# MLP of a two-layer encoder: two kinds of weight block sums move from accumulating DMAs to VectorE, up blocks go to other buffers, and the first chunk's work on h is spread further

## What is computed

```python
def sqrelu_mlp(h, w_up, w_down):
    return jnp.square(jax.nn.relu(h @ w_up)) @ w_down

for i in range(DEPTH):
    ...
    h = rmsnorm(x, g_ffn_pre[i])
    x = x + rmsnorm(sqrelu_mlp(h, mlp_w_up[i], mlp_w_down[i]), g_ffn_post[i])
```

## Time and profile before

| | us |
|---|---|
| median of 3 runs | 1190.64 (1189.11 to 1191.31) |
| profiled execution, its own time | 1189.05 |
| span in that profile | 1187.3 |
| TensorE busy (matmuls) | 1126.0 |
| VectorE busy | 912.2 |
| ScalarE busy | 763.1 |
| GpSimd busy | 317.0 |

### The profile page before, as it was taken

One profiled execution on the slowest core, in us unless ns is written; L12 is line 12 of the kernel. 1 busy time (PEld: TensorE's weight loads), 2 busy tenths in 40 slices (PEclk: granted clock), 3 DMA queues, 4 the chain that ended last, 5 costly groups with the idle time before them and its releaser, 6 DMA issues. The chain is left out here.

```text
span 1187.3 us, 18208 instructions
## 1 busy us (share of the span) xinstructions
PE 1126.0 (95%) x6462; PEld 976.4 (82%) x6462; DVE 912.2 (77%) x1328; ACT 763.1 (64%) x1266; POOL 317.0 (27%) x289
## 2 busy tenths in 40 slices
PE   8999999999899999899999999999998899899987
PEld 7788789887797897887977888879777887887876
DVE  5899965798586685679789888875897685585678
ACT  6778867556583583565787777775565673663754
POOL 5688850312022022112421111100311121030014
PEclk9999999999999999999999999999999999999999
DMA  5322134269579589575124322324669578687663
GB/s 162 105 60 71 36 109 106 72 186 200 143 174 214 137 188 206 120 206 107 54 54 103 75 70 62 97 64 122 199 143 210 131 180 186 159 177 171 157 175 103
DMA packets 142708, 157.22 MB, mean 132 GB/s; under 512 B 6269, under 2 KB 108669, under 8 KB 142122
## 3 DMA queue, kind: packets, MB, share of 16 engines
q1 hardware_dynamic: 112300, 109.68, 30.0%
q0 software_dynamic: 30256, 46.41, 23.6%
q10 hardware_dynamic: 78, 0.16, 0.0%
HBM read 147.58 MB, written 6.29 MB: 130 GB/s over the span
## 5 line engine op out<-in xcount | busy, mean ns | idle before, releaser
L2174 DVE TENSOR_TENSOR wlo<-mraw,whi 128x1024 fp32r<-128x1024 f32 x212 | 255.6, 1224 | 149.0 <-ACT whi L1509 148.9
L1509 ACT ACTIVATE whi<-mraw 128x1024 fp32r<-128x1024 f32 x212 | 218.1, 1053 | 195.2 <-DMA mraw<-in_mlp_w_down 108.3
L1203 PE MATMUL psum<-whi,aop_hi 128*128 128x512 f32 x448 | 178.6, 399 | 19.9 <-DVE wlo L2174 16.0
L1204 PE MATMUL psum<-wlo,aop_hi 128*128 128x512 f32 x448 | 174.7, 390 | 0.0
L1205 PE MATMUL psum<-whi,aop_lo 128*128 128x512 f32 x448 | 174.6, 390 | 0.0
L873 PE MATMUL psum<-hhi,whi 128*128 128x512 f32 x376 | 150.8, 401 | 0.8 <-DVE wlo L2163 0.5
L875 PE MATMUL psum<-hhi,wlo 128*128 128x512 f32 x376 | 147.0, 391 | 0.0
L874 PE MATMUL psum<-hlo,whi 128*128 128x512 f32 x376 | 146.8, 390 | 0.0
L1203 PEld LDWEIGHTS psum<-whi,aop_hi 128*128 128x128 f32 x448 | 84.1, 188 | 48.9 <-DVE wlo L2174 21.9
L1189 PE MATMUL psum<-hhi,whi 128*128 128x256 f32 x384 | 110.5, 288 | 14.4 <-DVE wlo L2174 12.1
L1190 PE MATMUL psum<-xlo,whi 128*128 128x256 f32 x384 | 109.3, 285 | 0.0
(11 more groups left out here) (314 smaller groups left out, 2807.9 us busy)
## 6 DMA issues: line engine op xcount, KB each, us to landing
mraw<-in_mlp_w_up SPq DMA_DIRECT2D x64, 512.0 KB, 6.8
mraw<-in_mlp_w_down SPq DMA_DIRECT2D x64, 512.0 KB, 4.9
mraw<-in_mlp_w_down POOLq DMA_DIRECT2D x60, 512.0 KB, 7.3
mraw<-in_mlp_w_up POOLq DMA_DIRECT2D x24, 512.0 KB, 10.7
wraw<-in_conv_pw_w SPq DMA_DIRECT2D x20, 512.0 KB, 4.5
wraw<-in_attn_w_in SPq DMA_DIRECT2D x16, 512.0 KB, 4.8
x_copy<-xT SPq DMA_DIRECT2D x2, 2048.0 KB, 7.4
xT<-x_copy SPq DMA_DIRECT2D x2, 2048.0 KB, 11.3
```

What stands on the lines that cost most here:

```text
L1203: pe.matmul(o, ah, wh, start=kt == 0 and (not kept or c == 0), stop=False)
L1204: pe.matmul(o, ah, wl, start=False, stop=False)
L1509: a.activation(split_unit(whi, e), raw_unit(l, c, e_), ACT.Copy).then_inc(s["m_hi"], 1)
L2174: d.tensor_tensor(split_unit(wlo, e), raw_unit(l, c, e_), split_unit(whi, e).bitcast(F32), ALU.subtract).then_inc(s["m_ready"], 1)
```

## The change

It has four parts.

1. **Sums.** Down P6 of chunks 0 to 2 and down P4 of chunks 1 and 2 are VectorE adds of blocks that lie in SBUF (`add_block`, now with the product as an argument), no longer accumulating DMAs. P4 of chunks 0 and 3 stays a DMA.
2. **Buffers and loads.** From chunk 2 on the up blocks B11 and B12 swap slots (B11 into that of down B21, B12 into that of down B22); B11 of chunk 1 and B12 of later ones are loaded behind P6's add, B11 of later ones behind P4's. `FIRST_SLOTS` of layer 0 is another permutation.
3. **GpSimd's order.** Chunk 0: P7, P5, P4. Later chunks: the up sums P7 and P4 first, then down P7h0, P5, P7h1. Chunk 3's P4 last.
4. **First chunk.** The 8 passes over h, the four sums and the forms' halves are placed later and further apart; three forms are finished by VectorE in the up part of chunk 1 or just ahead of it.

The functions `t_nth` and `v4_nth` only count semaphores anew. The core of the diff:

```diff
-FIRST_SLOTS = ((3, 1, 2, 0), (0, 1, 2, 3))
+FIRST_SLOTS = ((2, 3, 1, 0), (0, 1, 2, 3))
...
     d = down_slots(l, c - 1)
-    return d[B22], d[B12], d[B21], d[B11]
+    if c == 1:
+        return d[B22], d[B12], d[B21], d[B11]
+    return d[B21], d[B12], d[B22], d[B11]
...
-                    for b, at_ in ((B12, 3), (B11, 7), (B21, 11), (B22, 13)):
+                    for h in range(2):
+                        if c == 1:
+                            up_half(c, B12, h, n + 3 + h)
+                    for h in range(2):
+                        sp.wait_ge(s["t_sum"], t_nth(l, c - 1, "down", h))
+                        up_half(c, B11 if c == 1 else B12, h, n + 7 + h)
+                    for h in range(2):
+                        if c > 1:
+                            sp.wait_ge(s["t_sum"], t_nth(l, c - 1, "down", 2 + h))
+                            up_half(c, B11, h, n + 9 + h)
+                    for b, at_ in ((B21, 11), (B22, 13)):
...
-                for c in range(CHUNKS):
+                for h in range(2):
+                    add_down(l, 0, P7, h)
+                for i in (P5, P4):
                     for h in range(2):
-                        if c:
-                            add_up(l, c, P4, h)
-                        add_down(l, c, P7, h)
+                        add_down(l, 0, i, h)
+                for c in range(1, CHUNKS):
+                    for i in (P7, P4):
+                        for h in range(2):
+                            add_up(l, c, i, h)
+                    add_down(l, c, P7, 0)
                     for h in range(2):
                         add_down(l, c, P5, h)
-                    for h in range(2 if c < CHUNKS - 1 else 0):
-                        add_down(l, c, P6, h)
-                    for h in range(2 if c < CHUNKS - 1 else 0):
-                        add_up(l, c + 1, P7, h)
-                    for h in range(2):
-                        add_down(l, c, P4, h)
+                    add_down(l, c, P7, 1)
+                for h in range(2):
+                    add_down(l, CHUNKS - 1, P4, h)
...
-                for j, (kept_, forms) in enumerate(((P1, (A11, S7)), (P2, (A12,)), (P5, (S2,)), (None, (S5, A22)),
-                                                    (P6, (S4,)))):
+                for j, (kept_, forms) in enumerate(((P1, ()), (P2, ()), (P5, ()), (None, (A11, S7)), (P6, (A12, S2)))):
...
-            def add_block(l, h):
-
-                c = CHUNKS - 1
+            def add_block(l, c, i, h):
+
                 r = down_slots(l, c)
...
+                source, last_use = {P6: (B22, P5), P4: (B21, P6)}[i]
+                dve.wait_ge(*loaded(r[source], h, 2 * (CHUNKS * l + c) + 2))
+                dve.wait_ge(s["m_ready"], MLP_UNITS * l + DOWN[c] + DOWN_AT[c][last_use] + h + 1)
                 dve.wait_ge(v4_sum[h], 16 * v4_nth(l, c, "down", P5))
                 half = slice(h * D, (h + 1) * D)
                 to = mraw[:, r[B11], half]
...
+                d.tensor_tensor(to, to, mraw[:, r[source], half], ALU.add).then_inc(s["t_sum"], 1)
```

More of the change, by code:

```diff
@@ L91, in t_nth @@
 def t_nth(l, c, phase, k):
-    return 14 * l + (4 * c - 4 if phase == "up" else 12) + k + 1
+    return 24 * l + (8 * c - 6 if c else 0) + (4 if c and phase == "down" else 0) + k + 1
 def v4_nth(l, c, phase, i):
-    return 14 * l + 4 * c + (0 if phase == "up" else {P5: 1, P6: 2, P4: 3 if c < CHUNKS - 1 else 2}[i])
+    return 9 * l + 2 * c + (1 if phase == "up" else {P5: 2 if c else 1, P4: 3 if c else 2}[i])
 def v_nth(l, c, phase):
@@ L1502, in m_hi @@
                         act.wait_ge(v7_sum[h], 16 * v7_nth(l, c, "down", h))
-                    elif i == P6 and c == CHUNKS - 1:
+                    elif i == P6:
                         act.wait_ge(s["t_sum"], t_nth(l, c, "down", h))
-                    elif i in (P5, P6, P4):
+                    elif i == P4 and 0 < c < CHUNKS - 1:
+                        act.wait_ge(s["t_sum"], t_nth(l, c, "down", 2 + h))
+                    elif i in (P5, P4):
                         act.wait_ge(v4_sum[h], 16 * v4_nth(l, c, "down", i))
@@ L1889, in mlp @@
                 for i in range(4):
+                    if i == 3:
+                        m_hi(l, 8)
                     up_square(g, 2 * i)
@@ L1918, in mlp @@
                 m_hi(l, n + 16)
+                for form in (S5, A22, S4):
+                    form_hi_of(l, form)
                 for c in range(1, CHUNKS):
@@ L2518, in add_block @@
                 to = mraw[:, r[B11], half]
-                d.tensor_tensor(to, to, mraw[:, r[B22], half], ALU.add).then_inc(s["t_sum"], 1)
+                d.tensor_tensor(to, to, mraw[:, r[source], half], ALU.add).then_inc(s["t_sum"], 1)
             def add_up_block(l, c, i, h):
@@ L2657, in first_up @@
                 s_lo(g, 1)
-                for k in range(2):
-                    h_whole(l, k)
+                h_whole(l, 0)
+                h_whole(l, 1)
                 m_lo(l, 7)
@@ L2666, in first_up @@
                 relu(g, 6)
+                m_lo(l, 8)
                 s_lo(g, 2)
-                for k in range(2, 5):
-                    h_whole(l, k)
-                m_lo(l, 8)
+                h_whole(l, 2)
                 s7(g, 3)
+                a1_lo(g, 3)
                 m_lo(l, 9)
-                a1_lo(g, 3)
-                for k in range(5, KB):
-                    h_whole(l, k)
                 m_lo(l, 10)
@@ L2678, in first_up @@
                 s_sums(g, 3)
+                m_lo(l, 11)
                 a_lo(g, 3)
-                m_lo(l, 11)
                 s_lo(g, 3)
-                h_sum(l, S5)
+                h_whole(l, 3)
             def first_down(l):
@@ L2686, in first_down @@
                 m_lo(l, n + 4)
+                h_whole(l, 4)
+                h_whole(l, 5)
+                m_lo(l, n + 5)
+                add_block(l, 0, P6, 0)
+                m_lo(l, n + 6)
+                add_block(l, 0, P6, 1)
+                m_lo(l, n + 7)
+                h_whole(l, 6)
+                h_whole(l, 7)
+                m_lo(l, n + 8)
+                h_sum(l, S5)
+                m_lo(l, n + 9)
                 h_sum(l, S7)
-                m_lo(l, n + 5)
+                m_lo(l, n + 10)
                 h_sum(l, S2)
-                m_lo(l, n + 6)
                 h_sum(l, S4)
-                m_lo(l, n + 7)
+                m_lo(l, n + 11)
                 form_rest(l, A11)
-                m_lo(l, n + 8)
+                m_lo(l, n + 12)
                 form_rest(l, S7)
-                m_lo(l, n + 9)
+                m_lo(l, n + 13)
                 form_rest(l, A12)
-                m_lo(l, n + 10)
-                form_rest(l, S2)
-                m_lo(l, n + 11)
-                form_rest(l, S5)
-                m_lo(l, n + 12)
-                form_rest(l, A22)
-                m_lo(l, n + 13)
-                form_rest(l, S4)
                 m_lo(l, n + 14)
                 add_up_block(l, 1, P6, 0)
+                form_rest(l, S2)
                 m_lo(l, n + 15)
@@ L2710, in first_down @@
                 m_lo(l, n + 16)
+                form_rest(l, S5)
             def up_chunk(l, c):
                 g, n = CHUNKS * l + c, BASE[c]
-                for e in range(3, 8):
+                m_lo(l, n + 3)
+                if c == 1:
+                    form_rest(l, A22)
+                m_lo(l, n + 4)
+                if c == 1:
+                    form_rest(l, S4)
+                for e in range(5, 8):
                     m_lo(l, n + e)
@@ L2749, in down_chunk @@
                 m_lo(l, n + 5)
+                add_block(l, c, P6, 0)
                 m_lo(l, n + 6)
+                add_block(l, c, P6, 1)
                 add_product(g, P2)
@@ L2754, in down_chunk @@
                 m_lo(l, n + 9)
+                add_block(l, c, P4, 0)
                 add_product(g, P5)
                 m_lo(l, n + 10)
+                add_block(l, c, P4, 1)
                 m_lo(l, n + 11)
```

15 lines of the change are left out of this document (5 added, 10 removed).

## The result

The change takes 1137.84 us (median of 4 runs, 1136.93 to 1139.56), the kernel before in the same job 1189.88 (4 runs, 1188.16 to 1191.31). The ratio is 0.9565, 95% interval 0.9546 to 0.9583: 52 us or 4.35% faster. The profiled execution took 1139.56 us, the slowest of its four, with a span of 1137.8. Against the profiled pair of before (1189.05, span 1187.3) the gain is 49.5 us; the sum had said 46.3.

A forecast was written before the change was run, and what follows sets the result against it. The prediction took a queue of accumulating DMAs, not an engine, to bound the kernel. Terms 11.4 + 18.6 + 9.3 + 7.0 = 46.3 us off 1189.05 gave 1142.8, plus 1.6 to the median: 1144.4 us, range 1139.5 to 1157.

The forecast's parts named there:

- What bounds the kernel: MLP: TensorE's waits come from a queue of accumulating DMAs, not an engine; 50 us are there to win.
- The 0.27 us charged to each wait: TensorE's waits before MLP matmuls: each costs 0.27 us beyond its row; 39.8 us in 38 waits make 50 us.
- Down P4 and the next up part: Down P4 in chunks 1 and 2 and the next chunk's start: both kinds of wait go, winning 11.4 us.
- Up P4: Up chunks, P4 and P3: the sum is issued earlier and lands in 7 to 8 us, winning 18.6 us.
- 20.6, less 2 left: 18.6: Up P4 term: waits of 12.1 and 5.5 us plus 11 x 0.27 make 20.6; 2 us were expected to remain.
- The limit of 10.6: Up part: nothing is lost if the up P4 sum lands within 10.6 us of TensorE beginning the chunk.
- First chunk: First down chunk of each layer: waits at P2h1, P5h0 and P4's halves go, winning 9.3 us with 0.5 left.
- Last down half: Last down halves: P5's sums go ahead of P7h1's, ending `acc` and `wlo` waits, winning 7.0 us with 1.4 left.
- At nothing: Layer 0's first blocks in other slots, and B11 of chunks 2 and 3 loaded after P4's add: no cost.
- Rival 1: Up P4 sum stays slow and units lag in the packed first chunk: 8.5 us more, 1153 us; chance 20%.
- Rival 2: Start of up chunks: B12, loaded after P6's add, delays up P7's sum and TensorE waits; 1169 us; chance 8%.
- Rival 3: GpSimd cannot issue sums while VectorE adds, so they start only in VectorE's pauses; about 1198 us, slower; chance 2%.

The follow-up runs named there:

- e1: Kernel before with only GpSimd's sums reordered (down P4 ahead of the next up P7, P5 ahead of P7's second half); 1164.05 us, ratio 0.98.
- e8: The change with the up P4 sum's first half issued one unit later in layer 0, two in layer 1; 1153.84 us, ratio 0.9698.
- e10: Kernel before with GpSimd's new order, new form work places and both plain loads late in both layers, no new VectorE adds; 1139.2 us, ratio 0.9576.
- e9: Kernel before with only plain loads for the next down part issued later, one in layer 0, two in layer 1; 1187.65 us, ratio 0.9983.
- e12: e3 with the two plain loads behind the up P4 sum issued late, as in e10; 1147.56 us, ratio 0.9661.
- e4: The change with GpSimd's old order in later chunks: up P4 and down P7 sums alternating, both P7 halves ahead of P5; 1145.29 us, ratio 0.9639.
- e6: The change with `wlo` of down chunks 1 and 2 made in 2 pieces in layer 0, 8 in layer 1; 1147.53 us, ratio 0.9644.
- e3: The change with down P4 of chunks 1 and 2 summed by GpSimd DMAs again, ahead of the next up P7 sums; 1165.98 us, ratio 0.9809.
- e11: e3 with the two pairs of sums swapped, the next chunk's up P7 ahead of down P4; 1181.17 us, ratio 0.9933.
- e5: Kernel before with GpSimd's new order and the new places of the form work, all block sums still DMAs; 1152.38 us, ratio 0.9691.

## Why the prediction was right, and where it was off

**What bounds the kernel.** Right: with the waits for sums gone TensorE is busy 98% of the span, and the 22.4 us on VectorE cost nothing that shows. (TensorE's busy time, expected to stay near 1126 us, fell to 1116.8: first matmuls behind a wait are longer, and there was half clock.) The 0.27 us charged to each wait on top of its row held too: 39.8 us of waits less the 1.2 left, and 9.2 for the surcharge on 34 of them, make 47.8 against 49.8 in the parts.

**Down P4 and the next up part: right**, 11.9 us against 11.4. The diagnosis, a queue of accumulating DMAs, held, but adds on VectorE are only one way to mend it: e1 gets the same down parts by order alone.

**Up P4: the term that was mis-sized**, 21.7 us against 18.6. "20.6, less 2 left: 18.6" is the step of the sum that failed: 0.4 us were left and not 2, and the 20.6 was itself 1.6 short. The issue was forecast 0.7 us into the part and came at 0.7 to 1.5, the sum was wanted within 10.6, and it landed at 6.5 to 9.6. Even in up 1, issued at 3.6 and 3.9 and so later than the 2.4 forecast, it landed at 9.5 and 10.9: 0.4 us lost in one part. The limit of 10.6 was exact: landings at 10.2 (e8) and 10.5 (e10) cost nothing, 10.8 (e10) 0.3, and 10.9 (the change) 0.4. The prediction took landings of 7 to 8 us; four of the six took 5.8 to 5.9, the others 7.0 and 8.1. It kept 2 us because it could not tell why landings were 10 us in one place and 5.9 in another, though it named the two close loads in the earlier trace rows as a suspect. e9, e10 and e12 show it was them. The Trainium skill, "DMA: Bandwidth & Descriptors", section "Queues, rings and completion order", says that each DMA engine goes round among the queues that have work, packet by packet; landings of 5.9 to 7.3, 8.4 to 8.6 and 9.5 to 10.5 us with none, one and two plain loads close behind agree. The estimate from the fit in the same page of the Trainium skill, section "Anatomy of one DMA — SWDGE (gpsimd) path", that the prediction had weighed (3.2 us for 512 KB) is not seen: the quickest block sum of all these traces took 5.4 us (e1). The 1.6 us by which the 20.6 was short were a sixth delay at P4 and P3, in up 1 of layer 0, which stands in no wait row because TensorE was running at half clock (last section).

**First chunk: right**, 9.3 us against 9.3, with waits of 0.3 and 0.4 left at P5h0. But what waits there is ScalarE's copy of P1's product, not VectorE.

**Last down half: right**, 6.9 us against 7.0; e4, whose last down parts are 2.7 and 3.5 us longer, shows that GpSimd's order is worth 6 of it.

**At nothing: right.** B11 of chunk 2 is issued at 364.25 and 367.66 us, sooner than the 373 and 376 of the prediction, and landed after 6.1 and 7.4 us, ahead of the part that begins at 381.40.

**The sum and the range.** Measured less forecast, the terms missed by 0.5 us (down P4), 3.1 (up P4), 0.0 (first chunk) and -0.1 (last half): 3.5 together. The other 3 us are a second step that failed, from a profiled execution to a median: before's stood 1.6 us below its first median, and the prediction took the same of after, whose profiled execution stood 1.7 above, as the slowest of four. Neither error alone would have left the range. Its low end was too high by its own terms: with every left-over at nothing (2 + 0.5 + 1.4 us) the sum gives 1140.5, so 1139.5 allowed 1 us for all else, while before's three runs alone lay 2.2 us apart.

**The rivals.** Rival 1 (slow P4 sum, no slack) did not happen in the change, but e6 shows that VectorE is only some 4 us a part away from it. Rival 2 (B12 loaded late) did not either: the landing of up P7's sum ends no wait of VectorE's add behind it, since two sums share the engines there and not four. e3 and e11 show what becomes of late loads and sums when four do. Rival 3 (GpSimd kept from issuing) is refuted: VectorE is busy 35.26 of the 37 us from 266 to 303, most of it in `tensor_tensor` instructions, and the four sums of L761 from 261.4 to 286.1 landed after 5.8 to 7.1 us. That agrees with what the Trainium skill, "SBUF — State Buffer", section "Who interferes with whom", infers for `tensor_tensor`.

## What to carry to other kernels

When a transfer lands late in one place and early in another, list what other queues issue within a few us of it before pricing a change. Here one pair of plain loads, moved, was worth 13 us in the right order of sums (e5 to e10) and 0 in the wrong one (e9, where layer 0 had only one of the two moved; the form work stood where it was). Moving work off a queue can win somewhere else than where the work is: ask which later issue moves forward, and whether an engine that is ahead or catching up sets the spacing of others' DMAs. And take the low end of a range from the runs' spread as well as from the sum.

## What the runs showed that was not expected

A stall of TensorE can be followed by half clock. The kernel before, around the wait of 3.12 us ahead of P4 in up 1 of layer 0; columns are the stretch, its length, busy us and count of TensorE, its weight loads, VectorE, ScalarE and GpSimd, then the granted clock:

```profile
317.30:320.70 3.40, 3.40 (x30) 3.28 (x28) 0.00 (x0) 0.00 (x0) 0.00 (x0) 1.00 0.91 229
320.70:323.90 3.20, 0.09 (x1) 0.00 (x0) 1.28 (x2) 2.37 (x3) 0.00 (x0) 1.00 0.01 3
323.90:327.30 3.40, 3.40 (x16) 3.40 (x17) 3.37 (x4) 2.65 (x4) 0.00 (x0) 0.50 0.64 188
327.30:330.70 3.40, 3.40 (x30) 3.40 (x30) 3.37 (x5) 2.22 (x3) 1.19 (x1) 1.00 0.63 146
```

TensorE was full before, idle for 3.12 us, and then ran at a granted clock of 0.50 of full speed (1.2 GHz, the lower level) until 327.3, with half the matmuls in the same time. The unit took 4.47 us instead of 2.88. Such a delay of 1.6 us shows as busy time, not as a wait: of the 9.2 us by which TensorE's busy time fell from before to after, it is a part. In e3, whose four stalls before P4 were 3.2 to 4.1 us, it came with each, and for 6.8 us from 400.0 on:

```profile
400.00:403.40 3.40, 2.06 (x9) 2.07 (x10) 3.34 (x3) 3.37 (x6) 0.00 (x0) 0.50 0.21 56
403.40:406.80 3.40, 3.40 (x18) 3.40 (x17) 3.33 (x5) 1.87 (x3) 0.00 (x0) 0.50 0.71 252
```

In the MLPs of all these traces each of the 12 stalls of 3.1 us or more had such a stretch, and so had 5 of the 27 stalls of 1.5 to 2.7 us. The four of e11, two of e8 and one of e9 had 6.8 us of it each, so part of what these runs lose is clock and not the transfer that was late. In the change TensorE never stalls for 1.5 us in the MLP, and the clock stays at 1.00 there. So a long wait can cost half as much again as its row says, or more, and removing it gives that back.
